# Delta rule: v and output turned by whole-width block transposes and transfers through DRAM issued on ScalarE's queue; decay exponents by ScalarE

## The reference, cut to what matters

```
g = cumsum(g within a chunk of 64 tokens)
decay = exp(where(causal, g[..., :, None] - g[..., None, :], -inf))
a_mat = where(strict, einsum(k*beta, k) * decay, 0)
sol = triangular_solve(a_mat + I, concat([v*beta, k*beta*exp(g)]))
qk = einsum(q, k) * decay
# scan over chunks: o = (q*exp(g)) @ S + qk @ v_new ; S = S*exp(g_tot) + k_tail^T @ v_new
o = rms_norm(o, norm_w) * silu(z)        # then o @ w_branch_a
```

## Time and the profile before

| | |
|---|---|
| median of 3 executions | 1939.71 us |
| span of the profiled execution, first to last instruction | 1937.5 us |
| PE busy (matmuls) | 1922.7 us, 99% |
| DVE busy | 1365.1 us, 70% |
| ACT busy | 935.0 us, 48% |
| bodies of the delta rule | about 12 to 461 us of the span |
| granted TensorE clock, mean | 0.998 |

### The profile page before, as it was taken

One profiled execution on the slowest core, in us unless ns is written; L12 is line 12 of the kernel. 1 busy time (PEld: TensorE's weight loads), 2 busy tenths in 40 slices (PEclk: granted clock), 3 DMA queues, 4 the chain that ended last, 5 costly groups with the idle time before them and its releaser, 6 DMA issues.

```text
span 1937.5 us, 33061 instructions
## 1 busy us (share of the span) xinstructions
PE 1922.7 (99%) x11140; PEld 1581.1 (82%) x11140; DVE 1365.1 (70%) x1961; ACT 935.0 (48%) x1331; POOL 101.1 (5%) x296
## 2 busy tenths in 40 slices
PE   9999999999999999999999999999999999999997
PEld 7888887888888888888888888888888888888886
DVE  7779889797857777776566766577675466665556
ACT  6555565554455545455544445644443444443442
POOL 0102020010101111111000000000000000000000
PEclk9999999999999999999999999999999999999999
DMA  7444444444554545455655676555555555656555
GB/s 267 154 142 158 149 152 142 154 153 142 186 179 159 188 161 191 159 189 174 190 192 194 216 239 200 181 194 191 191 194 195 194 193 188 196 195 194 194 189 174
DMA packets 98013, 353.19 MB, mean 182 GB/s; under 512 B 10832, under 2 KB 11120, under 8 KB 97776
## 3 DMA queue, kind: packets, MB, share of 16 engines
q1 hardware_dynamic: 97904, 351.65, 55.4%
HBM read 349.51 MB, written 2.10 MB: 181 GB/s over the span
## 4 chain that ended last, share of the span: by engine, by line
PE 95%; DVE 2%; ACT 1%; issue 1%; DMA 1%; SPq 0%; DVEq 0%; ACTq 0%
PE pg L399 88%; PE B L399 5%; DVE gates L1212 1%; DMA raw<-in_weights 1%; PE B L493 0%; ACT whi L800 0%; DVE wlo L1204 0%; PE B L657 0%; ACT hraw L1086 0%; PE B L527 0%; ACT gates L1074 0%; PE B L666 0%; PE B L622 0%; ACT vda L1086 0%; ACT act_a L800 0%
## 5 line engine op out<-in xcount | busy, mean ns | idle before, releaser
L1204 DVE TENSOR_TENSOR wlo<-raw,whi 128x1024 fp32r<-128x1024 f32 (+1 forms) x640 | 779.4, 1221 | 452.1 <-ACT whi L800 433.8
L800 ACT ACTIVATE whi<-raw 128x1024 fp32r<-128x1024 f32 (+1 forms) x640 | 674.4, 1058 | 684.6 <-PE pg L399 673.0
L399 PE MATMUL pg<-whi,act_x 128*128 128x512 f32 x2960 | 950.5, 394 | 1.5 <-ACT whi L800 1.2
L399 PEld LDWEIGHTS pg<-whi,act_x 128*128 128x128 f32 x2960 | 555.3, 188 | 124.3 <-issue 8.9
L399 PE MATMUL pg<-wlo,act_x 128*128 128x512 f32 x1480 | 574.7, 390 | 0.0
L399 PE MATMUL pg<-whi,act_a 128*128 128x512 f32 x1632 | 504.8, 389 | 0.5 <-DVE act_a L1204 0.5
L399 PEld LDWEIGHTS pg<-whi,act_a 128*128 128x128 f32 x1632 | 306.3, 188 | 64.8 <-DVE act_a L1204 1.3
L399 PEld LDWEIGHTS pg<-wlo,act_x 128*128 128x128 f32 x1480 | 278.3, 188 | 53.3
L399 PE MATMUL pg<-wlo,act_a 128*128 128x512 f32 x816 | 317.5, 389 | 0.0
L399 PEld LDWEIGHTS pg<-wlo,act_a 128*128 128x128 f32 x816 | 153.2, 188 | 31.7
L399 PE MATMUL pg<-whi,act_b 128*128 128x512 f32 x512 | 158.4, 389 | 0.0
(11 more groups left out here) (230 smaller groups left out, 1106.5 us busy)
## 6 DMA issues: line engine op xcount, KB each, us to landing
raw<-in_weights SPq DMA_DIRECT2D x646, 512.0 KB, 3.8
gates<-in_ln_in SPq DMA_DIRECT2D x4, 512.0 KB, 5.9
gates<-in_ln_in SPq DMA_DIRECT2D x1, 2048.0 KB, 8.4
out<-gates SPq DMA_DIRECT2D x8, 256.0 KB, 2.8
raw<-in_weights SPq DMA_DIRECT2D x4, 256.0 KB, 4.6
cT<-in_xT SPq DMA_DIRECT2D x2, 512.0 KB, 7.2
qT<-in_xrow SPq DMA_DIRECT2D x2, 512.0 KB, 7.4
kT<-in_xrow SPq DMA_DIRECT2D x2, 512.0 KB, 6.3
```

The source lines that it names most:

```text
L399: return nc.tensor.matmul(o, l, r, start=start, stop=stop)
L800: return nc.scalar.activation(o, i, ACT.Copy, scale=scale)
L1204: return V.tensor_tensor(o, a, b, op)
```

## The change

Exponents: PE no longer multiplies `g_hi` and `g_lo`. In the prologue one small matmul more (`centre`, 128 by 32) gives the running sum of g in each chunk, measured from the chunk's middle, for all heads; ACT copies it to columns (`gc`), PE transposes it once, ACT copies the rows and sends them to DRAM. In each body one transfer, issued by ACT, spreads the eight rows of the body over all partitions into `decm` (512 KB in SBUF). ACT then makes max(0, own sum - row) in eight Relu of 128 by 128 and one Exp of 128 by 1024 with the sign turned. In bodies 1 to 3 this lies in slots 4 to 7, in body 0 in slots 13 and 14.

v: one DVE transpose of 128 by 1024 (32 by 32 blocks, in place within their partitions) in slot 20 into `stage`; ACT issues a transfer of `stage` to DRAM in slot 21, waits for it in slot 23 and issues four transfers back, each to 32 partitions, which put the blocks in their places. `v_scaled` reads the result in slots 26 and 30. o: the same with two DVE transposes of 128 by 512 in slot 11, transfers in slots 12 and 14, ACT's copy in slot 24 and DVE's subtraction in slot 25.

```diff
-OT_TURN = {11: 3, 12: 4, 14: 2, 18: 1, 20: 3, 21: 3}
-OT_HI = 29
-V_TURN = {21: 1, 22: 3, 23: 3, 27: 3, 28: 2, 29: 2, 30: 1, 31: 1}
+O_BLOCKS, V_BLOCKS = 11, 20
+O_HI = 24
+V_SCALED = (26, 30)
-ROWS = range(2, 6)
+DECAY = range(4, 8)
...
+        turn_v, turn_o = (nc.dram_tensor(n, (4, SB, 4, 8 * SB), F32).ap() for n in ("turn_v", "turn_o"))
+        sums_out = nc.dram_tensor("sums_out", (NB, 8 * P), F32).ap()
...
@@ PE
+                    mm(B[3][:, 64:96], centre, g_all[:, :]).then_inc(N["pe_sc0"], 1)
+                if s == 9:
+                    pe.wait_ge(N["act_gc"], 1)
+                    nc.tensor.transpose(B[3][0:SB, P:2 * P], pz[:, 1, :], ident).then_inc(N["pe_gT"], 1)
...
-                if s == 12:
-                    pe.wait_ge(N["rows"], 1 + j + 1)
-                    if isinstance(j, int):
-                        pe.wait_ge(N["act_glo"], 1)
+                if s == 13:
+                    pe.wait_ge(N["act_silu"], 1 + 3 * j + 1)
                     pe.wait_ge(N["dve_conv"], 1 + 6 * j + 2)
                     pe.wait_ge(N["act_sqq"], 1 + j)
-                    for t in range(TOK):
-                        mm(B[1 + t][:, :], after_r[:, :], flat(g_hi[:, 4 * t:4 * t + 4, :]), True, False)
-                        last = mm(B[1 + t][:, :], after_r[:, :], flat(g_lo[:, 4 * t:4 * t + 4, :]), False, True)
-                    last.then_inc(N["pe_dt"], 1)
-                if s == 13:
-                    pe.wait_ge(N["act_silu"], 1 + 3 * j + 1)
-                    pe.wait_ge(N["act_decay"], 1 + j + 1)
...
@@ ACT
+                    for t in range(TOK):
+                        by_t = B[3][:, 64 + HEADS * t:64 + HEADS * (t + 1)].rearrange("p (j h) -> p j h", h=HB)
+                        a0 = SC["gc"][0] + 4 * t
+                        copy(scal[:, :, a0:a0 + 4], by_t)
+                        last = copy(pz[:, 1, :].rearrange("p (j t h) -> p j t h", j=NB, t=TOK)[:, :, t, :], by_t)
+                    last.then_inc(N["act_gc"], 1)
+                    act.wait_ge(N["pe_gT"], 1)
+                    copy(sums[0:SB, :], B[3][0:SB, P:2 * P]).then_inc(N["act_gT"], 1)
+                    act.wait_ge(N["act_gT"], 1)
+                    act.dma_start(sums_out.rearrange("j (i c) -> (j i) c", c=P), sums[0:SB, :]).then_inc(sums_kept, 16)
+                if s == 10:
+                    act.wait_ge(sums_kept, 16)
+                    sums_in(0)
+            def sums_in(j):
+                act.wait_ge(N["dve_qk"], 1 + 2 * j)
+                act.dma_start(flat(decm[:, :, :]), sums_out[bass.ds(j, 1)].rearrange("o c -> (o c)").partition_broadcast(P)
+                              ).then_inc(sums_full, 16)
+            def past(j, part, parts):
+                if part == 0:
+                    act.wait_ge(sums_full, 16 * (j + 1))
+                    act.wait_ge(N["dve_g"], 1 + j + 1)
+                for i in range(8 // parts * part, 8 // parts * (part + 1)):
+                    last = nc.scalar.activation(decm[:, i, :], decm[:, i, :], ACT.Relu, bias=gcur[:, i:i + 1], scale=-1.0)
+            def decay(j):
+                act.wait_ge(N["act_past"], 1 + j + 1)
+                nc.scalar.activation(decm[:, :, :], decm[:, :, :], ACT.Exp, scale=-1.0).then_inc(N["act_decay"], 1)
             def dn_build(j, s):
-                if s in ROWS and not isinstance(j, int):
...
-                    for i in range(per * (s - ROWS[0]), per * (s - ROWS[0] + 1)):
-                        last = nc.scalar.activation((g_hi if i < 8 else g_lo)[:, i % 8, :], c("same"), ACT.Copy,
-                                                    scale=gcur[:, i:i + 1])
...
-                if s == 12:
-                    act.wait_ge(N["pe_dt"], 1 + j + 1)
-                    act.wait_ge(N["dve_qk"], 1 + 2 * j)
-                    for t in range(TOK):
-                        last = nc.scalar.activation(decm[:, 4 * t:4 * t + 4, :], B4[1 + t], ACT.Exp)
-                    last.then_inc(N["act_decay"], 1)
+                if s == 0 and not isinstance(j, int):
+                    sums_in(j)
+                if s in DECAY and not isinstance(j, int):
+                    past(j, s - DECAY[0], len(DECAY))
+                    if s == DECAY[-1]:
+                        decay(j)
+                if s == 13 and isinstance(j, int):
+                    past(j, 0, 1)
...
+                if s == 14 and isinstance(j, int):
+                    decay(j)
+            def blocks_out(scratch, kept):
+                act.dma_start(scratch.rearrange("a x b c -> (a x) (b c)"), stage[:, :, :, :].rearrange("p b q x -> p (b q x)")
+                              ).then_inc(kept, 16)
+            def blocks_in(scratch, dst, full):
+                for b in range(4):
+                    act.dma_start(dst[b * SB:(b + 1) * SB], scratch[:, :, b].rearrange("a x (q i) -> x a q i", i=SB)
+                                  ).then_inc(full, 16)
+            def v_moves(j, s):
+                if s == V_BLOCKS + 1:
+                    act.wait_ge(N["dve_vS"], 1 + j + 1)
+                    blocks_out(turn_v, v_kept)
+                if s == V_BLOCKS + 3:
+                    act.wait_ge(v_kept, 16 * (j + 1))
+                    blocks_in(turn_v, vtok, v_full)
...
@@ DVE
-                    tt(g_hi[:, :, :], rep(c("same"), 8), bc(gcur[:, 0:8], P), ALU.mult).then_inc(N["rows"], 1)
...
+                if s == V_BLOCKS:
+                    dve.wait_ge(N["act_silu"], 1 + 3 * j + 2)
+                    if not isinstance(j, int):
+                        dve.wait_ge(o_kept, 16 * j)
+                    V.transpose(stage[:, :, :, :].rearrange("p b q x -> p q b x"),
+                                cT[:, 1].rearrange("p h (q b x) -> p (h q) b x", q=TOK, x=SB)).then_inc(N["dve_vS"], 1)
+                if s in V_SCALED:
+                    if s == V_SCALED[0]:
+                        dve.wait_ge(N["pool_rinv"], 1 + j + 1)
+                        dve.wait_ge(v_full, 64 * (j + 1))
+                    v_scaled(j, V_SCALED.index(s))
...
+                if not alone and s == O_BLOCKS:
+                    dve.wait_ge(N["dve_oh"], 1 + 2 * j + 2)
+                    dve.wait_ge(v_kept, 16 * (j + 1))
+                    for t in range(TOK):
+                        last = V.transpose(stage[:, :, :, :].rearrange("p b (h t) x -> p h t b x", t=TOK)[:, :, t],
+                                           od[:, t].rearrange("p h (b x) -> p h b x", x=SB))
+                    last.then_inc(N["dve_oS"], 1)
```

More of the change, by code:

```diff
@@ L91 @@
 NPARAM = _at
-SC = {"beta": (0, 8), "eg": (8, 16), "tail": (16, 24), "g": (24, 32), "glo": (32, 40)}
+SC = {"beta": (0, 8), "eg": (8, 16), "tail": (16, 24), "gc": (24, 32)}
 NSC = 40
@@ L135, in build @@
         zs = tmp("zs", [P, 2, NG])
-        g_hi, g_lo = (dn.enter_context(nc.sbuf_tensor(n, [P, 8, P], F32R)) for n in ("g_hi", "g_lo"))
-        g_r = dn.enter_context(nc.sbuf_tensor("g_r", [P, TOK * HEADS], F32R))
+        stage = tmp("stage", [P, 4, 8, SB])
+        oT = tmp("oT", [P, 4, 8, SB])
         dn.close()
@@ L220, in build @@
         warm = flat(TTf[:, :, :])
+        centre, sums = (flat(QKT[:, :, :])[:, i * P:(i + 1) * P] for i in range(2))
+        vtok = flat(kT[:, :, :]).rearrange("p (a q x) -> p a q x", a=4, x=SB)
+        turn_v, turn_o = (nc.dram_tensor(n, (4, SB, 4, 8 * SB), F32).ap() for n in ("turn_v", "turn_o"))
+        sums_out = nc.dram_tensor("sums_out", (NB, 8 * P), F32).ap()
         def xt(a, b):
@@ L260, in build @@
         const_full = sem("const_full")
+        sums_kept = sem("sums_kept")
+        sums_full = sem("sums_full")
+        v_kept, v_full, o_kept, o_full = (sem(n) for n in ("v_kept", "v_full", "o_kept", "o_full"))
         ln_full = sem("ln_full")
@@ L295, in __call__, with by_block, by_source @@
                 self.until(self.mark(ins))
+        def by_block(dst):
+            return dst.rearrange("p h (t a x) -> p (h t) a x", t=TOK, x=SB)
+        def by_source(blocks):
+            return blocks[:, :, :, :].rearrange("p a q x -> p q a x")
         def hi(buf, k, n, t0=0, t1=SEQ):
@@ L969, in dn_scan @@
                     copy(hi(act_a, HB * j, HB, t * P, (t + 1) * P), B4[2 + t]).then_inc(N["act_oT"], 1)
-                if not alone and s == OT_HI:
-                    act.wait_ge(N["dve_od"], 1 + j + 1)
-                    copy(hi(act_a, HB * j, HB), qT[:, :, :]).then_inc(N["act_oT"], 2)
+                if not alone and s == O_HI:
+                    act.wait_ge(o_full, 64 * (j + 1))
+                    copy(by_block(hi(act_a, HB * j, HB)), by_source(oT)).then_inc(N["act_oT"], 2)
             def body(n, evac_fn, mixes=()):
@@ L1278, in prologue @@
                     pro(ts(c("same"), c("after"), -1.0, ALU.mult, 1.0, ALU.add))
-                    V.tensor_copy(after_r[:, :], c("after"))
+                    pro(ts(centre, c("same"), c("same")[:, CH - 1:CH], ALU.subtract))
                     lv = vda[:, 0, 0:4 * CH].rearrange("p (a b d) -> p a b d", a=2, b=2)
@@ L1475, in dn_scan @@
```

(18 more changed lines are left out.)

82 lines of the change are left out of this document (30 added, 52 removed).

## The result

The changed kernel takes 1943.78 us (median of 10 executions, 1942.05 to 1946.28) against 1940.09 for the kernel before on the same chip (10 executions, 1938.97 to 1940.74). The ratio is 1.0022, with a 95% interval of 1.0014 to 1.003: a loss of 0.2%, small but clear of the noise. I had forecast 1937.0, with a range of 1935.5 to 1940.0: the gain of PE that I had counted was outweighed by a loss that I had not. The profile is of one execution, which took 1944.35 us.

What follows compares the result with a forecast made beforehand. PE's queue was taken as the bound: -3.72 us of matmuls removed, +0.25 added, +0.3 for slot 7 and +0.5 for body 0 give -2.7 us, so 1937.0 us from 1939.71, with a range of 1935.5 to 1940.0.

Steps and rivals of the forecast that it cites:

- What bounds the kernel: Whole kernel: PE's queue is the bound; DVE or ACT time counts only if hand-overs to PE come late.
- PE's sum, -3.5 us: PE, four bodies: removed matmuls give -3.72 us, one matmul and one transpose added in body 0 cost 0.25.
- Slot 7: ACT, bodies 1 to 3: Relu, table load and Exp just fit before k's evacuation; 0.3 us lost in all.
- Body 0: Sums' round trip and spread tile before slot 13 make the squares late; PE stalls 0.2 to 0.7 us, taken as 0.5.
- The round trips: Transfers of v and o through DRAM: about 4 us to land, covered in the slots between, no cost.
- the output's cover: Slots 12 to 14: 5 to 6 us for o's store to land, then ten slots.
- DVE, zero: DVE, four bodies: some 39 us less busy time, worth zero; the new transposes cost zero too.
- C: Slots 14 and 23: ACT waits for stores' landing in every body; 1948.8 us at the slowest row, chance 0.07.
- D's late tile in body 0: Body 0: late sums cost 3 us (or slot 7 misses by 1 us a body); 1939.2 to 1940.2, chance 0.12.

Runs made afterwards that it cites:

- the first experiment: The changed kernel with the output's rounding and subtraction back in slots 29 and 30 and the first v_scaled moved from slot 26 to 27; 1936.29 us, ratio 0.9983.
- the run of the decay exponents alone: The changed kernel's new exponents, with v and o turned by 16 small DVE transposes each as in the kernel before; 1937.16 us, ratio 0.9986.
- The run with more DVE work: The changed kernel plus an unread row sum of 1.21 us on DVE ahead of slot 25's subtraction in bodies 1 to 3; 1948.48 us, ratio 1.0046.

## Why the prediction was wrong

**What bounds the kernel:** right. PE's queue is the bound; to within about 1 us the runs moved by what was taken from it, what made it wait and what its clock lost.

**PE's sum, -3.5 us:** right; four matmuls a body put back cost 3.7 us, and the kernel without the new waits gains 3.4 by the medians. By the two profiled executions it is 2.9 us: from the first tile matmul of body 0 to the first one behind body 3 there are 452.85 us in the kernel before and 449.91 in the first experiment. The two instructions added on PE in body 0 hold it for 0.22 and some 0.12 us, 0.34 in all where I had 0.25.

**Slot 7:** right, and as near as worked out: the evacuation of k ended at 264.80 and PE took it at 265.05 in body 2, 0.25 us later, where I had 263.2 and 263.44 (answer to the earlier trace rows):

```profile
263.73 1.07 ACT L900 ACTIVATE hraw<-pg 128x512 f32<-128x512 f32 x2
...
265.05 1.05 PE L511 MATMUL B<-cst,hraw 128*128 128x128 f32 x8
```

**Body 0:** the way was right, the stall of 0.5 us was not there. The squares began at 53.43, as worked out, but PE came to the product at 55.91, not at 55.0, with no wait on the list. In this execution PE had lost 0.58 us against the kernel before in the first two slots; and my reading had moved PE forward and held ACT still. From the squares' end to the product it is 0.5 us in the kernel before (55.20 and 55.72), in the kernel after (55.43 and 55.91) and in the run of the decay exponents alone, where both come earlier (54.83 and 55.35). The transfers on this path were 2.0 us for the 16 KB where I had 3.1, and 6.9 us for the spread tile in body 0 where I had 3.3 to 5.7 from its nearest rows; it landed at 50.7, 0.4 us before ACT came to it at 51.09.

**The round trips:** right in what they cost, which is nothing. Stores landed in 3.5 and 3.9 us (medians; 5.0 at most) where I had put 4. DVE has no wait for them; ACT has 2.6 us of waits for the output's transposes in three bodies, and no wait of PE follows from them. But the output's cover was not the 5 to 6 us I had: in each of the three bodies the first load back is issued as soon as the store has landed (in body 1 the store at 163.77, the load at 167.68), so a slower store would have held ACT's queue in slot 14. The Trainium skill ("Perfetto Trace Analysis", section "DMA Instruction — HWDGE (DVE, Sync)") says that the completion of a write to HBM can be surprisingly long. No run here shows that: these stores of 512 KB took about as long as the weight loads of the same size beside them (3.5 us, the median of bodies 1 to 3).

**DVE, zero: the step that failed.** I wrote that DVE's worth is zero on both sides, since "each transpose is done in a slot where DVE idles or did the old ones". I summed what DVE does and looked at where its *new* instructions stand, and left out the two *old* ones that the change moves: the subtraction of o, from slot 30 to 25, and the first `v_scaled`, from 31 to 26. The diff shows both in its constants, and the prediction even names `v_scaled` near 329, but only as the time by which the loads must have landed. It had asked for a check of each hand-over that moves; the one from q's convolution over SiLU and the `Pm` copies to PE's slot 28 was not checked. Neither instruction is longer than before, and DVE as a whole is 44 us lighter; but in slots 25 and 26 DVE had a full place, the end of the inverse (8.1 us from 436.60 on in the kernel before, in which it idled 0.4), and q's last convolution stands behind. Its lateness had at most 0.2 us of room until PE (0.69 us became a wait of 0.7, 1.22 us one of 1.0), because on ACT the `Pm` copies are queued behind the SiLU that waits for it. What I put at zero measured 5.8 us of waits and, in the profiled execution, 1.7 us of clock behind them. In the kernel before, the chain shows only as ACT's 2.91 us wait for `cT`, which the prediction never looked at and which looks like room.

**The size** then closes, best in the traces. Over the four bodies (first tile matmul of body 0 to the first one behind body 3) the kernel after takes 457.40 us and the first experiment's 449.91: 7.5 us more, which is 5.8 us of waits and one stretch at the lower clock of 1.7. The run with more DVE work takes 461.40, 11.5 more, where its waits and two stretches are 8.4 + 3.4 = 11.8. The medians agree: 1936.29 + 5.8 + 1.7 = 1943.8, measured 1943.78, and 1936.29 + 8.4 + 2 x 1.7 = 1948.1, measured 1948.48; that the first of them is met so closely is chance, as not every execution has one stretch. The ten executions fit the clock only in part: those with a mean clock of 0.998 took 1942.05 to 1943.79 us, those with 0.997 took 1943.50 to 1946.28, the one with 0.996 took 1945.24. What makes up the rest of the spread is open.

**The rivals:** none had this mechanism. C, the one on the slower side, had the right kind (something on ACT held up with work behind it) but at slot 23 and from a store; the point from which it decides, 7.8 us, was not reached. D's late tile in body 0 came nearest of what was foreseen and stayed 0.4 us short of holding ACT up.

## What to carry to other kernels

Where one engine's queue is the bound and the others run just ahead of it, an instruction that is moved counts like one that is added: take each constant of slots in the diff, list what stands behind the new place on that engine, and follow it over the next engine's queue to the bound, before summing busy time. Idle time of an engine is room only if what it waits for is not itself on such a chain; here 2.91 us of ACT's idle time were none. And when a wait can't be removed, look at what else is queued behind it: exchanging two items in ACT's slot 27 gave back all that the moved work had cost (1935.85 us, against 1936.29 with the work itself moved back).

## What the runs showed of the hardware that I had not expected

A single wait of PE of 1.7 us, in a stream that is otherwise without a gap, was followed in one of three bodies by a stretch at the lower of the two clock levels, worth another 1.7 us; with a wait of 2.1 us (and one of 0.4 us 9.5 us earlier) in two of three; with waits of 1.0 us or less in none. So a wait's price on PE can be double its length. The times of the changed kernel also spread more, 4.2 us between its ten executions and 1.3 to 2.4 in the eleven of each kernel with shorter waits or none, of which the clock explains a part.

A DVE block transpose of 128x1024 took 1.20 us and one of 128x512 0.69, no more than DVE's arithmetic instructions of the same columns (1.22 and 0.69):

```profile
L1468 DVE STREAM_TRANSPOSE stage<-cT 128x1024 f32<-128x1024 f32 x4 | 4.8, 1202 | 0.0
L1522 DVE STREAM_TRANSPOSE stage<-od 128x512 f32<-128x512 f32 x6 | 3.9, 685 | 0.0
```

so the 16 transposes of 32x256 for v (7.0 us) became one of 1.2 us, for a round trip through DRAM that cost PE nothing here, with the output's part of it just in cover.
